# Norms that end the mixers, taken for half the tokens at a time beside the output projection, which begins with the other mixer's rows

## The reference, cut to what matters

```
layer 0:
  a_out = rglru(...)
  o     = gated_delta_rule(...)                       # 4 heads of 128
  b_out = rms_norm(o, norm_g) * silu(z)
  mix   = concat([a_out, b_out]) @ w_out0
layer 1:
  o     = rwkv7_scan(...)                             # 8 heads of 64
  o     = (o - mean(o)) * rsqrt(var(o) + 64e-5) * lnx_g + lnx_b
  c_out = (o + bonus) * g
  mix   = concat([c_out, mla(...)]) @ w_out1
x = layer_norm(ALPHA * x + mix)
x = layer_norm(ALPHA * x + conv_ffn(x)); x = x + sigmoid(x Wg + bg) * (p Wp)
```

## Time and profile before

| what | us |
|---|---|
| median of 3 runs | 3918.93 (3916.99 to 3925.47) |
| profiled execution, its own time | 3921.35 |
| profiled execution, span | 3919.6 |
| TensorE busy | 3528.7 (90% of the span) |
| VectorE busy | 1900.4 (48%) |
| GpSimd busy | 1192.2 (30%) |
| ScalarE busy | 1067.7 (27%) |
| mean granted clock of TensorE | 0.957 of full speed |

### The profile page before, as it was taken

How to read it: one execution, slowest core, us unless ns; L and a number is a source line. 1 busy time by engine, 2 the same in 40 slices (tenths; PEclk the granted TensorE clock), 3 DMA queues, 4 the chain that set the end, 5 groups by cost and what they waited for, 6 DMA issues and landing times.

```text
span 3919.6 us, 74126 instructions
## 1 busy us (share of the span) xinstructions
PE 3528.7 (90%) x31266; PEld 3368.8 (86%) x31266; DVE 1900.4 (48%) x2402; ACT 1067.7 (27%) x1495; POOL 1192.2 (30%) x562
## 2 busy tenths in 40 slices
PE   8998787799999999989997876777699999999979
PEld 7997787799999999989996445777599999999979
DVE  1563554375454454655412225545447544544564
ACT  2365232242111111241013334222324111111142
POOL 2332532353333333333332000000064333333323
PEclk9999999899999999999998998998899999999989
DMA  3111000221111111112221016121121111111111
GB/s 126 57 52 52 1 0 24 83 65 49 43 43 43 43 43 43 49 56 84 91 72 47 1 43 214 36 43 35 65 99 51 43 43 43 43 43 43 43 44 70
DMA packets 106406, 212.49 MB, mean 54 GB/s; under 512 B 58560, under 2 KB 59840, under 8 KB 105600
## 3 DMA queue, kind: packets, MB, share of 16 engines
q1 hardware_dynamic: 94832, 168.65, 13.8%
q10 hardware_dynamic: 11408, 41.34, 2.7%
HBM read 172.73 MB, written 37.23 MB: 54 GB/s over the span
## 4 chain that ended last, share of the span: by engine, by line
PE 82%; ACT 6%; DVE 6%; issue 4%; DMA 1%; POOL 0%; ACTq 0%; DVEq 0%; SPq 0%; PEldq 0%; POOLq 0%
PE PS L727 56%; PE PS L744 8%; PE PS L1333 6%; PE PS L992 4%; PE PS L1298 1%; PE PS L1397 1%; ACT XH L1654 1%; ACT Y L1655 1%; PE PS L1356 1%; PE PS L1276 1%; DVE XL L2193 1%; PE PS L1273 1%; PE PS L758 0%; PE PS L1258 0%; PE PS L920 0%
## 5 line engine op out<-in xcount | busy, mean ns | idle before, releaser
L727 PE MATMUL PS<-XH,WHI 128*128 128x274 f32 x4320 | 1254.7, 290 | 11.4 <-ACT RN L1549 6.3
L727 PE MATMUL PS<-XL,WHI 128*128 128x274 f32 x4320 | 1254.0, 290 | 0.0
L727 PE MATMUL PS<-XH,WLO 128*128 128x274 f32 x4320 | 1252.0, 290 | 0.0
L843 POOL TENSOR_TENSOR WHI<-RAW,EPS 128x1024 fp32r<-128x1024 f32 x234 | 454.4, 1942 | 2452.5 <-PE PS L727 1417.4
L727 PEld LDWEIGHTS PS<-XH,WHI 128*128 128x128 f32 x4320 | 817.6, 189 | 14.4 <-issue 8.0
L727 PEld LDWEIGHTS PS<-XL,WHI 128*128 128x128 f32 x4320 | 819.2, 190 | 0.0
L727 PEld LDWEIGHTS PS<-XH,WLO 128*128 128x128 f32 x4320 | 818.5, 189 | 0.0
L846 POOL TENSOR_TENSOR WLO<-RAW,WHI 128x1024 fp32r<-128x1024 f32 x234 | 605.0, 2586 | 18.4
L727 PE MATMUL PS<-HH,WHI 128*128 128x274 f32 x1280 | 372.0, 291 | 0.0
L727 PE MATMUL PS<-HH,WLO 128*128 128x274 f32 x1280 | 370.4, 289 | 0.0
L727 PE MATMUL PS<-HL,WHI 128*128 128x274 f32 x1280 | 369.5, 289 | 0.0
(11 more groups left out here) (440 smaller groups left out, 5676.4 us busy)
## 6 DMA issues: line engine op xcount, KB each, us to landing
RAW<-in_units SPq DMA_DIRECT2D x234, 512.0 KB, 3.5
prepared_rows<-PREP SPq DMA_DIRECT2D x8, 1096.0 KB, 5.4
CIN<-prepared_rows SPq DMA_DIRECT2D x17, 512.0 KB, 4.5
c_rows<-DX ACTq DMA_DIRECT2D x14, 548.0 KB, 2.8
RKV<-c_rows SPq DMA_DIRECT2D x4, 1644.0 KB, 11.0
X<-in_x SPq DMA_DIRECT2D x8, 548.0 KB, 9.0
XR<-in_x ACTq DMA_DIRECT2D x8, 548.0 KB, 11.8
bonus_gate_rows<-BG SPq DMA_DIRECT2D x4, 1096.0 KB, 5.0
```

Source lines behind the costliest of these rows:

```text
L727: last = nc.tensor.matmul(PS[:, 4 * slot + b, 0:width], wt[:, ring, w], r[:, k, b * width:(b + 1) * width], start=n == 0, stop=n == 3 * nk ...
L843: nc.gpsimd.tensor_tensor(WHI[:, s, :], RAW[:, s, :], ZERO.to_broadcast([128, 1024]), ALU.add)\
```

## The change

The norm of the recurrent mixer is taken in two halves of the tokens, each for all four tiles. The first half (`o_rows(0, ...)`, `f_rows(0, ...)`) stands where the whole norm stood. The second half is spread over the first units of the output projection: TensorE takes its sums after units 1 to 4 (`o_second_half`, `f_second_half`), VectorE's rows come after its work on unit 5 and unit 6, and a wait for `mix_ready` 8 stands ahead of the projection of the second half of the tokens. For units 0 and 1 TensorE first takes the four tiles of the other mixer (`EARLY`), of both units, and then the four of this mixer (`LATE`), waiting for each. Logarithm and exponential of the first half run on two tiles at a time (1096 columns), those of the second half on one tile for the logarithm and on two for the exponential.

All low parts are now VectorE's. In layer 0 z is loaded as two transfers. In layer 1 bonus and gate are loaded by SyncE as two transfers of four tiles each, ahead of its loop over the chunks, into room that `XH` and `XL` take later. The state outputs and the load of x into `XR` are issued by ScalarE ahead of the norm, not behind it, and VectorE waits for the state outputs before `layer_end`.

```diff
@@ -557,11 +559,16 @@
+        LATE, EARLY = ((4, 5, 6, 7), (0, 1, 2, 3)), ((0, 1, 2, 3), (4, 5, 6, 7))
         SECOND_OUT, SECOND_UP = (6, 7, 0, 1, 2, 3, 4, 5), (2, 3, 0, 1)
         POOL_LOWS = 4
         def row_half(x, h):
             return x[:, 2 * BW * h:2 * BW * (h + 1)]
+        def row4_half(x, h):
+            return x[:, :, 2 * BW * h:2 * BW * (h + 1)]
@@ -746,17 +753,19 @@
-        def matmul_half_rows(place, ring, nk, hi, lo, h, row_ready):
-            for k in range(nk):
+        def matmul_half_rows(place, ring, nk, hi, lo, h, row_ready, rows_of=None, first=True, last_rows=True):
+            order = list(range(nk)) if rows_of is None else list(rows_of)
+            for k in order:
                 row_ready(k)
                 w = slice(k * 128, (k + 1) * 128)
                 for b in range(2):
                     t = slice((2 * h + b) * BW, (2 * h + b + 1) * BW)
                     for n, (wt, r) in enumerate(((WHI, hi), (WHI, lo), (WLO, hi))):
                         last = nc.tensor.matmul(PS[:, 2 * place + b, 0:BW], wt[:, ring, w], r[:, k, t],
-                                                start=k == 0 and n == 0, stop=k == nk - 1 and n == 2)
+                                                start=first and k == order[0] and n == 0,
+                                                stop=last_rows and k == order[-1] and n == 2)
             return last
@@ -811,6 +820,8 @@
             sp.dma_start(MB[1][:, :, :], io["s_c"]).then_inc(c_state_in, 16)
+            for rows4, first, n in ((BONUS4, 0, 0), (GATE4, 4, 1)):
+                sp.dma_start(rows4, BROW.rearrange("(k m) p n -> p (k m) n", m=4)[:, first:first + 4, :]).then_inc(mix_in[n], 16)
             with sp.Fori(0, 7) as i:
@@ -820,11 +831,6 @@
-            sp.wait_ge(c_act[0], C_ACT.at(C_SAMPLE, "o"))
-            for m in range(4):
-                if m >= 2:
-                    sp.wait_ge(f_dve, F_DVE.at(m - 2, "gated"))
-                sp.dma_start(BGL[m % 2][:, :, :], BROW.rearrange("(k m) p n -> m p k n", m=4)[m]).then_inc(f_in[m % 2], 16)
             load_units(OUT_UNIT[1] // 2 + 2, NU // 2)
@@ -886,9 +892,6 @@
-            for h in range(2):
-                pool.wait_ge(xh_ready, 8 + h + 1)
-                nc.gpsimd.tensor_tensor(XL[:, 4 + h, :], OT[:, h, :], XH[:, 4 + h, :], ALU.subtract).then_inc(mix_ready[0], 1)
             def low(n):
@@ -1053,14 +1056,54 @@
...
+            def o_squares_summed(h, m, place):
+                pe.wait_ge(o_square, 4 * h + m + 1)
+                for b in range(2):
+                    last = nc.tensor.matmul(PS[:, 2 * place + b, 0:BW], ONES, ON[h][m // 2][:, m % 2, b * BW:(b + 1) * BW],
                                             start=True, stop=True)
                 last.then_inc(o_sum, 1)
+            def o_first_half():
+                for m in range(4):
+                    o_squares_summed(0, m, m)
+                pe.wait_ge(norm_read, 11)
+            def o_second_half(m):
+                if 1 <= m < 5:
+                    pe.wait_ge(norm_read, 12 + m - 1)
+                    o_squares_summed(1, m - 1, 3)
+            def f_averaged(h, m, place):
+                for b in range(2):
+                    t = (2 * h + b) * BW
+                    last = nc.tensor.matmul(PS[:, 2 * place + b, 0:BW], PAIR_ONES, CO[:, m, t:t + BW], start=True, stop=True)
+                last.then_inc(f_mean, 1)
+            def f_squares_summed(h, m, place):
+                pe.wait_ge(f_act, F_ACT.at(h, m, "square"))
+                for b in range(2):
+                    last = nc.tensor.matmul(PS[:, 2 * place + b, 0:BW], PAIR_ONES, SQC[h][m // 2][:, m % 2, b * BW:(b + 1) * BW],
+                                            start=True, stop=True)
+                last.then_inc(f_var, 1)
+            def f_first_half():
+                for m in range(4):
+                    f_averaged(0, m, m)
+                for m in range(4):
+                    f_squares_summed(0, m, m)
+                for m in range(4):
+                    pe.wait_ge(f_act, F_ACT.at(0, m // 2, "log"))
+                    f_averaged(1, m, m)
+                pe.wait_ge(f_dve, F_DVE.at(1, 1, "centred"))
+            def f_second_half(m):
+                if 1 <= m < 5:
+                    if m == 1:
+                        pe.wait_ge(f_dve, F_DVE.at(1, 3, "centred"))
+                    else:
+                        pe.wait_ge(f_act, F_ACT.at(1, m - 2, "log"))
+                    f_squares_summed(1, m - 1, 3)
@@ -1092,18 +1135,27 @@
-                pe.wait_ge(mix_ready[l], 4)
                 if l == 0:
                     pe.wait_ge(rg_split, 8)
-                with pe.Fori(0, 3) as i:
-                    for s in range(2):
-                        pe.wait_ge(unit_split, first + 2 * i + s + 1)
-                        pe.wait_ge(out_read, 2 * i + s + 1 + 18 * l)
-                        matmul_half(s, s, 0, 8, XH, XL, 0).then_inc(unit_done, 1)
+                (o_first_half, f_first_half)[l]()
+                for m in range(2):
+                    pe.wait_ge(unit_split, first + m + 1)
+                    pe.wait_ge(out_read, m + 1 + 18 * l)
+                    matmul_half_rows(m, m, 8, XH, XL, 0, lambda k: None, EARLY[l], True, False)
+                for m in range(2):
+                    matmul_half_rows(m, m, 8, XH, XL, 0, lambda k: pe.wait_ge(mix_ready[l], LATE[l].index(k) + 1), LATE[l], False, True)\
+                        .then_inc(unit_done, 1)
+                    (o_second_half, f_second_half)[l](m)
+                for m in range(2, 6):
+                    pe.wait_ge(unit_split, first + m + 1)
+                    pe.wait_ge(out_read, m + 1 + 18 * l)
+                    matmul_half(m % 2, m % 2, 0, 8, XH, XL, 0).then_inc(unit_done, 1)
+                    (o_second_half, f_second_half)[l](m)
                 for m in (6, 7):
                     pe.wait_ge(unit_split, first + m + 1)
                     pe.wait_ge(out_read, m + 1 + 18 * l)
                     matmul_half(m % 2, m % 2, 0, 8, XH, XL, 0).then_inc(half_done, 1)
+                pe.wait_ge(mix_ready[l], 8)
                 for q, m in enumerate(SECOND_OUT):
@@ -1422,21 +1474,6 @@
             pe.wait_ge(c_dve[0], C_DVE.at(C_SAMPLE, "m"))
...
             layer_end(1)
@@ -1603,32 +1640,41 @@
             act.wait_ge(o_zeroed, 1)
...
+            for h in range(2):
+                act.dma_start(row4_half(ZT, h), ZROW.rearrange("t p n -> p t n")[:, :, 2 * BW * h:2 * BW * (h + 1)]).then_inc(mix_in[h], 16)
             for k in range(8):
                 act.dma_start(XR[:, k, :], io["x"][:, k, :]).then_inc(x_in[k // 2], 16)
             def o_squares(h):
...
+                for m in range(4):
+                    nc.scalar.activation(ON[h][m // 2][:, m % 2, :], row_half(OT[:, m, :], h), ACT.Square).then_inc(o_square, 1)
+            def o_roots(h, q):
+                act.wait_ge(norm_read, 10 + (q + 1 if h == 0 else 2 + 2 * q + 2))
+                nc.scalar.activation(ON[h][q][:, :, :], ON[h][q][:, :, :], ACT.Exp, scale=-0.5).then_inc(o_root, 1)
+            def o_high(h):
+                for m in range(4):
+                    act.wait_ge(o_gated, 4 * h + m + 1)
+                    nc.scalar.activation(row_half(XH[:, 4 + m, :], h), row_half(OT[:, m, :], h), ACT.Copy).then_inc(xh_ready, 1)
+            o_squares(0)
+            nc.scalar.activation(EPS[:, 5:6], EPS[:, 0:1], ACT.Ln, bias=1.0)
+            for q in range(2):
+                act.wait_ge(o_sum, 2 * q + 2)
+                nc.scalar.activation(ON[0][q][:, :, :].rearrange("p m (b n) -> p (m b) n", b=2), banks(q), ACT.Ln, bias=EPS[:, 1:2],
+                                     scale=1 / 128).then_inc(norm_read, 1)
+            for q in range(2):
+                o_roots(0, q)
+            o_high(0)
+            o_squares(1)
+            for m in range(4):
+                act.wait_ge(o_sum, 4 + m + 1)
+                nc.scalar.activation(rows(ON[1][m // 2][:, m % 2, :]), duo(3), ACT.Ln, bias=EPS[:, 1:2], scale=1 / 128)\
                   .then_inc(norm_read, 1)
...
+            for q in range(2):
+                o_roots(1, q)
+            o_high(1)
             act.wait_ge(state_out, 32)
@@ -1962,28 +2008,44 @@
...
             for n, (out, p, j) in enumerate((("s_c_p", 1, (0, 7)), ("s_c_s", 0, C_SAMPLE))):
                 act.wait_ge(c_dve[p], C_DVE.at(j, "m"))
                 act.dma_start(io[out], MB[n][:, :, :]).then_inc(c_state_out, 16)
...
             for k in range(8):
                 act.dma_start(XR[:, k, :], XROW[:, k, :]).then_inc(x_in[k // 2], 16)
+            def f_squares(h):
+                for m in range(4):
+                    act.wait_ge(f_dve, F_DVE.at(h, m, "centred"))
+                    nc.scalar.activation(SQC[h][m // 2][:, m % 2, :], row_half(CO[:, m, :], h), ACT.Square).then_inc(f_act, 1)
+            def f_roots(h, q):
+                act.wait_ge(f_act, F_ACT.at(h, q if h == 0 else 2 * q + 1, "log"))
```

(116 more changed lines are left out.)

79 lines of the change are left out of this document (4 added, 75 removed).

## The result

The changed kernel takes 3885.87 us (median of 4 runs, 3883.02 to 3888.06); the kernel before, on the same chip, 3919.91 us (4 runs, 3916.99 to 3925.47). The ratio is 0.991, 95% interval 0.9897 to 0.9924: 34 us faster. The profiled execution took 3884.71 us, span 3882.9 against 3919.6: 36.7 us.

A forecast was written before the change was run, and what follows sets the result against it. TensorE, 82% of the span, was taken as the bound. Gains of 6.4 us (layer 0) and 8.7 (layer 1), 15.1 in all, take the profiled 3921.35 to 3906.2, median 3904; range 3896 to 3913.

The forecast's parts named there:

- The held start: Both layers: early rows wait for VectorE's `layer_end` increment, so only half width gains; 3904 us, chance 0.72.
- Half widths, units, VectorE's run: Norms and output projection: shorter half-width steps, then VectorE's run of 14.35 us (layer 0) and 17.9 (layer 1).
- The clock, layer 0: Start of layer 0's second half of tokens: TensorE's clock falls after 2.2 us idle, costing 2.5 us.
- The sum for the change itself: Both layers' gains together: 6.4 + 8.7 = 15.1 us, or 17.6 without layer 0's clock fall.
- These 90 us are all that the change can touch: Stretches from last chunk work to first output-projection matmul, 41.6 us in layer 0 and 48.7 in layer 1, bound any gain.
- The early rows run early after all: Rival, both layers: the release doesn't bind, early rows start at 692.6 and 2803; 3885 us, chance 0.05.
- Tokens late behind the bonus load: Rival, layer 1's first chunks: tokens wait behind the moved loads, up to 11 us, 3915; chance 0.03.

The follow-up runs named there:

- the two written-out kernels: Kernel before and changed kernel, each with TensorE's layer 1 chunk loop written out, without a branch back: 3884.89 us and 3868.24 us.
- the early-release kernel: Changed kernel with VectorE's `out_read` increment moved from the head of `layer_end` to ahead of the first half's rows, both layers: 3864.96 us, ratio 0.9861.

## Why the prediction was right and wrong

- **The held start: right.** The first row matmul came 26.1 us behind the chunks in layer 0 (26.2 predicted) and 27.1 in layer 1 (27.1), released by the increment at `layer_end`. Two experiments show it: the order of rows is worth nothing while it is held, and moving the increment alone gives 20.9 us, 17.4 of them in the two stretches.
- **Half widths, units, VectorE's run: right.** From the end of unit 5 to the second half 14.2 us (14.35) in layer 0, 17.9 (17.9) in layer 1; idle 1.85 (2.2) and 5.57 (5.7). The held rows cost 2.4 us in layer 0 (1.12 and 2.81 against 0.78 and 0.73), where 2.75 were counted.
- **The clock, layer 0: wrong.** I took a fall behind 2.2 us of idleness. The idle time was 1.85 us and no fall came; behind 5.57 us in layer 1 it came (window, PE, PEld, DVE, ACT, POOL, granted clock):

```profile
761.15:762.35 1.20, 1.20 (x9) 1.20 (x10) 1.17 (x2) 0.00 (x0) 0.00 (x0) 1.00 0.06 14
2849.95:2851.15 1.20, 1.20 (x5) 1.20 (x6) 1.17 (x2) 0.00 (x0) 0.00 (x0) 0.50 0.00 0
```

  That term was mis-sized by 2.5 us. The Trainium skill's bound on idle gaps ("TensorE: Matmul & The Clock Gate", "Why this matters for your kernels") came out right in layer 0; it still doesn't cover the 0.50 behind 2.27 us in the earlier trace rows.
- **The sum for the change itself: right.** 15.1 us predicted (17.6 without that fall), 16.7 measured between the two written-out kernels.
- **"These 90 us are all that the change can touch": this step failed.** It took the change's reach to be the stretches where its instructions run. The change also lengthened TensorE's program ahead of a loop of 1,798 instructions, and three of that loop's six stalls went: 13.4 us by the windows, 14.0 in the kernel before with nothing but the loop shifted. The chain's "issue 4%" in the earlier trace rows was the row to ask about, though the six stalls' 19.6 us are only a small part of its some 157. With this term the forecast would have been 3904 less 14, or 3890, and without layer 0's fall of the clock 3887.5, against 3885.87 measured.
- **A rival right in its number alone.** "The early rows run early after all" was given 3885, and the result is 3885.87. That figure was itself a slip: 3921.35 less its 36.1 us is the profiled execution's time, and on the median, as the forecast was put, it gives 3883. The trace rules it out: the rows didn't run early. When they were let run early the time was 3864.96.
- **Tokens late behind the bonus load: absent**, as costed at nothing; moving the loads back changed nothing.

## What to carry to other kernels

Before a change is costed, look up in the trace the "issue" idle rows of every long loop on the bounding engine: a change anywhere ahead of such a loop can shift its code and move the time by as much as the change itself. To know what a change is worth, compare it also with the loop written out (or shifted) in both kernels. And where a statement only says "this buffer is free", put it where the buffer becomes free, not at the head of the next phase: here the reordering gave nothing until that one line was moved (what the line gives without the reordering was not run).

## What the runs showed of the hardware

- With a loop of 1,798 TensorE instructions the engine stood still for 3.0 to 4.0 us at the head of every turn or of every second one, depending on the loop's place. Some 1.4 us of this stays when the loop is written out, but a lower clock follows each stall, and each costs 4.8 us (14.4 for three, after against before) to 5.7 (17.2 for three, after against its written-out loop). Written out, no wait over 1.4 us was left in the loop, with 59 instruction packets against 68.
- 129 increments of a semaphore on TensorE ahead of a wait of 14.9 us made it 24.6 us.
- The length of the last gap alone didn't settle TensorE's clock. It stayed at 1.00 behind 1.85 us of idleness. Behind the stall of 3.46 us at 2584.52 before, it was still 1.00 in the next 1.0 us, and 0.50 behind 1.22 us more of idleness at 2587.51. And two shorter gaps close together, 1.26 and 1.07 us with six matmuls between them in the early-release kernel, left it at the lower level (1.00 between them, 0.50 in the 1.4 us from 701.60 on):

```profile
701.60 0.60 PE L766 MATMUL PS<-XH,WHI 128*128 128x274 f32 x1 [1.07 <-DVE XL L2218]
701.99 0.43 PE L766 MATMUL PS<-XL,WHI 128*128 128x274 f32 x1
```
